# NSA loop in 32 steps of two heads each, and the merge's projection in three split passes

## What is computed

```
q, kv, gates, q_gla, k_gla, v_gla, ..., g_merge = split(rmsnorm(x) @ w_in)
o_a = gate0 * compressed_attention + gate1 * softmax(q_rot k_slc^T) v_slc + gate2 * softmax(q_rot k_win^T) v_win
o_b = rmsnorm(gated linear attention) * silu(r)
gate_a, gate_b = split(sigmoid(g_merge))
merged = gate_a * (o_a @ w_up_nsa) + gate_b * (o_b @ w_up_gla)
x = x + merged @ w_out, then the last SwiGLU layer and the final norm
```

## Time and profile before

| | |
|---|---|
| median of 3 runs | 2349.17 us (2347.92 to 2351.39) |
| the profiled execution's own time | 2335.24 us |
| its span | 2333.4 us |
| mean granted clock of TensorE | 0.981 of full |
| PE busy | 2231.5 us, 96% of the span |
| POOL, DVE, ACT busy | 1146.1, 1003.0, 861.6 us |
| HBM read | 187.92 MB |

### The profile page before, as it was taken

How to read it: one execution, slowest core, us unless ns; L and a number is a source line. 1 busy time by engine, 2 the same in 40 slices (tenths; PEclk the granted TensorE clock), 3 DMA queues, 4 the chain that set the end, 5 groups by cost and what they waited for, 6 DMA issues and landing times.

```text
span 2333.4 us, 28069 instructions
## 1 busy us (share of the span) xinstructions
PE 2231.5 (96%) x10194; PEld 1803.3 (77%) x10194; DVE 1003.0 (43%) x1605; ACT 861.6 (37%) x1239; POOL 1146.1 (49%) x623
## 2 busy tenths in 40 slices
PE   4899989999998999899999999999799999999997
PEld 3788868888886988788888888878556668888886
DVE  5366556422424047744422446353683215331432
ACT  4576744322323223334322334443353224222222
POOL 3777755554554455435554554643101335654552
PEclk9999999999999999999999999999799999999999
DMA  3212213332332222123332332322101223332332
GB/s 131 62 57 62 63 46 100 91 112 85 97 107 67 90 82 73 55 81 104 91 110 88 94 110 77 112 64 73 45 1 46 90 91 91 99 111 84 95 107 73
DMA packets 53251, 193.26 MB, mean 83 GB/s; under 512 B 6816, under 2 KB 7728, under 8 KB 52912
## 3 DMA queue, kind: packets, MB, share of 16 engines
q1 hardware_dynamic: 50688, 184.95, 25.3%
q10 hardware_dynamic: 2480, 7.19, 0.8%
HBM read 187.92 MB, written 4.19 MB: 82 GB/s over the span
## 4 chain that ended last, share of the span: by engine, by line
PE 78%; DVE 9%; ACT 7%; issue 4%; POOL 2%; DMA 0%; SPq 0%; DVEq 0%; ACTq 0%; POOLq 0%
PE ps L367 21%; PE ps L368 20%; PE ps L369 20%; PE ps L934 2%; PE ps L878 2%; PE ps L901 1%; PE ps L572 1%; PE ps L574 1%; PE ps L573 1%; DVE arena L1726 1%; PE ps L458 1%; PE ps L888 1%; ACT w_split L952 1%; PE ps L629 1%; PE ps L631 1%
## 5 line engine op out<-in xcount | busy, mean ns | idle before, releaser
L1401 POOL TENSOR_TENSOR w_split<-ring,w_split 128x1024 fp32r<-128x1024 f32 (+2 forms) x319 | 820.9, 2574 | 1010.7 <-ACT w_split L952 1010.7
L952 ACT CAST w_split<-ring 128x1024 fp32r<-128x1024 f32 (+2 forms) x319 | 347.9, 1091 | 1052.3 <-PE ps L369 931.6
L367 PE MATMUL ps<-u_split,w_split 128*128 128x512 f32 x1768 | 707.5, 400 | 23.8 <-POOL w_split L1401 11.0
L369 PE MATMUL ps<-u_split,w_split 128*128 128x512 f32 x1768 | 694.1, 393 | 0.0
L368 PE MATMUL ps<-u_split,w_split 128*128 128x512 f32 x1768 | 693.5, 392 | 0.0
L367 PEld LDWEIGHTS ps<-u_split,w_split 128*128 128x128 f32 x1768 | 335.3, 190 | 104.2 <-issue 20.4
L369 PEld LDWEIGHTS ps<-u_split,w_split 128*128 128x128 f32 x1768 | 335.0, 189 | 71.4
L368 PEld LDWEIGHTS ps<-u_split,w_split 128*128 128x128 f32 x1768 | 335.5, 190 | 70.1 <-issue 2.9
L367 PE MATMUL ps<-hid,w_split 128*128 128x512 f32 x648 | 254.4, 393 | 2.8 <-DVE arena L1860 2.8
L368 PE MATMUL ps<-hid,w_split 128*128 128x512 f32 x648 | 252.8, 390 | 0.0
L369 PE MATMUL ps<-hid,w_split 128*128 128x512 f32 x648 | 252.7, 390 | 0.0
(11 more groups left out here) (283 smaller groups left out, 2554.4 us busy)
## 6 DMA issues: line engine op xcount, KB each, us to landing
ring<-in_w_hgrn SPq DMA_DIRECT2D x32, 512.0 KB, 3.6
ring<-in_w_attn_qk SPq DMA_DIRECT2D x24, 512.0 KB, 3.6
ring<-in_w_merge SPq DMA_DIRECT2D x24, 512.0 KB, 3.4
ring<-in_w_gu0a SPq DMA_DIRECT2D x22, 512.0 KB, 3.6
ring<-in_w_gu0b SPq DMA_DIRECT2D x22, 512.0 KB, 3.5
ring<-in_w_gu1a SPq DMA_DIRECT2D x22, 512.0 KB, 3.6
ring<-in_w_gu1b SPq DMA_DIRECT2D x22, 512.0 KB, 3.6
ring<-in_w_gu2a SPq DMA_DIRECT2D x22, 512.0 KB, 3.5
```

The source lines that it names most:

```text
L367: nc.tensor.matmul(ps[:, bank], ws[:, 0, r, w], act[:, 0, c], start=c == 0, stop=False)
L369: m = nc.tensor.matmul(ps[:, bank], ws[:, 1, r, w], act[:, 0, c], start=False, stop=c == n - 1)
L952: nc.scalar.copy(ws[:, 0, slot, 0:w], ring[:, r, 0:w]).then_inc(s["w_hi"], 1)
L1401: nc.gpsimd.tensor_tensor(ws[:, 1, slot, 0:w], ring[:, r, 0:w], ws[:, 0, slot, 0:w].bitcast(F32), ALU.subtract).then_inc(s["w_lo"], 1)
```

## The change

The NSA loop has 32 steps (p, x, tt): a pair of heads, a branch and one query tile. The pairs are (0, 5), (1, 4), (2, 7), (3, 6): the first head's features stand in rows 0 to 63, the second's in rows 64 to 127, and one's number is even and the other's odd, so that their values go to different column halves of the array and their outputs to different halves of one bank. The query tiles come in the order 3, 0, 2, 1. A step's scores take one bank for each head; three pairs of banks go round, so scores run two steps ahead, and they wait for the copy of step e-3. In a step VectorE makes one mask addition and one negated maximum for both heads, one reciprocal, and two scalings by two per-partition scalars (reciprocal and gate) in one instruction; ScalarE makes two exponentials and one copy; TensorE two score matmuls, 2(tt+1) transposes and 2(tt+1) value matmuls of 128 columns that alternate between the heads. `nsa_add` runs for both heads of a pair after its eight steps.

In the merge the third unit becomes a split one with 24 passes. `goT` and `oaT` are split once, ScalarE making the hi halves (`outputs_hi`, four inside the loop at steps 4 to 7, two at steps 20 and 22, two after the loop) and GpSimd the lo halves. The staging of the weights in the merge goes from two units for each j to three. Loops of ScalarE and VectorE over the heads are written out.

In the diff old bodies that the listing above shows are left out.

```diff
@@ -61,7 +61,7 @@
...
-PLAIN = [("mid", k) for k, name in enumerate(MID) if name[0] == "w"] + [("merge", 3 * j + 2) for j in range(DC)]
+PLAIN = [("mid", k) for k, name in enumerate(MID) if name[0] == "w"]
...
@@ -226,12 +226,17 @@
...
-        nmax, nneg, nsum, nrec, nw = [take(2, TT) for _ in range(5)]
+        nneg, nsum, nrec = [take(3, 2) for _ in range(3)]
...
+        oa_hi = nc.alloc_sbuf_tensor_at("oa_hi", [P, 4, T], R32, offset=arena_at + 4 * 18 * T)
+        go_hi = nc.alloc_sbuf_tensor_at("go_hi", [P, HEADS_G, T], R32, offset=arena_at + 4 * 44 * T)
+        oa_lo = nc.alloc_sbuf_tensor_at("oa_lo", [P, 4, T], R32, offset=arena_at + 4 * 32 * T)
+        go_lo = nc.alloc_sbuf_tensor_at("go_lo", [P, HEADS_G, T], R32, offset=arena_at + 4 * 28 * T)
...
@@ -240,10 +245,18 @@
...
-        prob, probT = [shared[:, k * 2560:(k + 1) * 2560].rearrange("p (a n) -> p a n", a=2) for k in range(2)]
-        OFF = [0, P, 3 * P, 6 * P]
-        KOFF = [0, 4 * P, 7 * P, 9 * P]
-        BOFF = [0, P, 512, 1024]
+        prob = shared[:, 0:3072].rearrange("p (a h n) -> p a h n", a=3, h=2)
+        probT = shared[:, 3072:5120].rearrange("p (a h n) -> p a h n", a=2, h=2)
+        STEPS = [(p, x, tt) for p in range(HEADS_N // 2) for tt in (3, 0, 2, 1) for x in range(2)]
+        PAIR = [(p, HEADS_N // 2 + (p ^ 1)) for p in range(HEADS_N // 2)]
+        UP_ORDER = (0, 2, 1, 3)
+        OA_DONE = {0: 3, 2: 4, 1: 7, 3: 8}
+        def step_banks(e, n):
+            return ps[:, 2 * (e % 3):2 * (e % 3) + 2, 0:n * P]
...
@@ -867,56 +880,56 @@
             def nsa_scores(e):
...
+                p, x, tt = STEPS[e]
+                if e < 3:
                     pe.wait_ge(s["oa_ready"], 4)
                 else:
...
+                    pe.wait_ge(s["npt_ready"], e - 2)
+                for k, hh in enumerate(PAIR[p]):
+                    rows = slice(k * HD, k * HD + HD)
+                    m = nc.tensor.matmul(step_banks(e, tt + 1)[:, k], q_n[rows, hh % 4, tt * P:(tt + 1) * P],
                                          k_n[rows, x, 0:(tt + 1) * P], start=True, stop=True)
                 m.then_inc(s["ns_ps"], 1)
             def nsa_transposes(e):
...
+                _, _, tt = STEPS[e]
+                for k in range(2):
+                    pe.wait_ge(s["ns_scaled"], 2 * e + k + 1)
+                    for b in range(tt + 1):
+                        m = nc.tensor.transpose(step_banks(e, tt + 1)[:, k, b * P:(b + 1) * P],
+                                                prob[:, e % 3, k, b * P:(b + 1) * P], ident[:])
                 m.then_inc(s["nt_ps"], 1)
             def nsa_values(e):
...
+                p, x, tt = STEPS[e]
+                pe.wait_ge(s["npt_ready"], e + 1)
+                if p >= 2:
+                    pe.wait_ge(s["oa_acc"], 2 * p - 2)
+                for b in range(tt + 1):
+                    for k, hh in enumerate(PAIR[p]):
+                        vcols = slice(x * P + k * HD, x * P + k * HD + HD)
+                        rows = slice(hh % 2 * HD, hh % 2 * HD + HD)
+                        m = nc.tensor.matmul(ps[rows, 6 + p % 2, tt * P:(tt + 1) * P], vsw[:, b, vcols],
+                                             probT[:, e % 2, k, b * P:(b + 1) * P],
+                                             start=x == 0 and b == 0, stop=x == 1 and b == tt)
                 m.then_inc(s["no_ps"], 1)
             pe.wait_ge(s["nrope"], 6)
             pe.wait_ge(s["o_scaled"], HEADS_H + HEADS_G)
...
+            E = len(STEPS)
             nsa_scores(0)
+            nsa_scores(1)
             for e in range(E):
...
+                if e + 2 < E:
+                    nsa_scores(e + 2)
                 nsa_transposes(e)
                 if e:
                     nsa_values(e - 1)
             nsa_values(E - 1)
...
+            pe.wait_ge(s["npt_ready"], E)
             for j in range(DC):
                 b = 4 * (j % 2)
                 pe.wait_ge(s["merged"], j + 1)
@@ -924,15 +937,16 @@
...
-                if j == 0:
-                    pe.wait_ge(s["gb_ready"], HEADS_G)
-                    pe.wait_ge(s["oa_acc"], HEADS_N)
-                rr, v = ring_use("merge", 3 * j + 2)
-                pe.wait_ge(w_ready[rr], v)
-                for c in range(8):
-                    src = oaT[:, c] if c < 4 else goT[:, c - 4]
-                    m = nc.tensor.matmul(ps[:, b + 2 + c // 4], ring[:, rr, c * P:(c + 1) * P], src,
-                                         start=c % 4 == 0, stop=c % 4 == 3)
+                rr, v, _ = split_use("merge", 3 * j + 2)
+                pe.wait_ge(s["w_lo"], v)
+                for n, c in enumerate((4, 5, 6, 7) + UP_ORDER):
+                    if j == 0:
+                        pe.wait_ge(s["up_lo"], n + 1)
+                    up, low = (go_hi, go_lo) if c >= 4 else (oa_hi, oa_lo)
+                    o, w = ps[:, b + 2 + c // 4], slice(c * P, (c + 1) * P)
+                    nc.tensor.matmul(o, ws[:, 0, rr, w], up[:, c % 4], start=n % 4 == 0, stop=False)
+                    nc.tensor.matmul(o, ws[:, 0, rr, w], low[:, c % 4], start=False, stop=False)
+                    m = nc.tensor.matmul(o, ws[:, 1, rr, w], up[:, c % 4], start=False, stop=n % 4 == 3)
...
@@ -1348,37 +1362,49 @@
                 nc.scalar.copy(oaT[:, ft], ps[:, ft]).then_inc(s["oa_ready"], 1)
             act.dma_start(h, a["h_spill"]).then_inc(s["reloaded"], 16)
...
+            def nsa_exps(e):
+                p, x, tt = STEPS[e]
+                act.wait_ge(s["ns_neg"], e + 1)
+                for k in range(2):
+                    nc.scalar.activation(prob[:, e % 3, k, 0:(tt + 1) * P], step_banks(e, tt + 1)[:, k], ACT.Exp,
+                                         bias=nneg[:, e % 3, k:k + 1], accum_out=nsum[:, e % 3, k:k + 1]
                                          ).then_inc(s["ns_exp"], 1)
...
+            def nsa_copies(e):
+                n = STEPS[e][2] + 1
+                act.wait_ge(s["nt_ps"], e + 1)
+                nc.scalar.copy(probT[:, e % 2, :, 0:n * P], step_banks(e, n)).then_inc(s["npt_ready"], 1)
+            def outputs_hi(n):
+                f = n if n < HEADS_G else UP_ORDER[n - HEADS_G]
+                if n < HEADS_G:
+                    act.wait_ge(s["nrope"], 6)
+                    act.wait_ge(s["gb_ready"], f + 1)
+                else:
+                    act.wait_ge(s["oa_acc"], OA_DONE[f])
+                dst, src = (go_hi, goT) if n < HEADS_G else (oa_hi, oaT)
+                nc.scalar.copy(dst[:, f], src[:, f]).then_inc(s["up_hi"], 1)
+            nsa_exps(0)
+            nsa_exps(1)
+            for e in range(len(STEPS)):
+                nsa_copies(e)
+                if e + 2 < len(STEPS):
+                    nsa_exps(e + 2)
+                if 4 <= e < 4 + HEADS_G:
+                    outputs_hi(e - 4)
+                if e in (20, 22):
+                    outputs_hi(HEADS_G + (e - 20) // 2)
+            outputs_hi(HEADS_G + 2)
+            outputs_hi(HEADS_G + 3)
             for j in range(DC):
                 for k in range(2):
...
+                    ahead("merge", 3 * j + k)
                     act.wait_ge(s["mg_raw"], 2 * j + k + 1)
                     nc.scalar.activation(msig[:, 2 * (j % 2) + k], msig[:, 2 * (j % 2) + k], ACT.Sigmoid
                                          ).then_inc(s["mg_sig"], 1)
+                ahead("merge", 3 * j + 2)
                 act.wait_ge(s["m_full"], j + 1)
                 nc.scalar.copy(hid[:, 0, j], mtmp[:, j % 2]).then_inc(s["m_hi"], 1)
             early_norm(6, "mix_out", "gu2a")
@@ -1565,9 +1591,14 @@
...
+            for n in range(2 * HEADS_G):
+                pool.wait_ge(s["up_hi"], n + 1)
+                f = n if n < HEADS_G else UP_ORDER[n - HEADS_G]
+                low, up, src = (go_lo, go_hi, goT) if n < HEADS_G else (oa_lo, oa_hi, oaT)
+                nc.gpsimd.tensor_tensor(low[:, f], src[:, f], up[:, f].bitcast(F32), ALU.subtract).then_inc(s["up_lo"], 1)
...
-                for k in range(2):
-                    lo("merge", 3 * (j + 1) + k) if j + 1 < DC else lo("mix_out", k)
+                for k in range(3):
+                    ahead("merge", 3 * j + k)
...
@@ -2143,61 +2174,44 @@
                 times_sin(x)
                 add_sin(x)
...
+            def nsa_stats(e):
+                n = STEPS[e][2] + 1
+                dve.wait_ge(s["ns_ps"], e + 1)
+                diag = step_banks(e, n)[:, :, (n - 1) * P:n * P]
+                nc.vector.tensor_tensor(diag, diag, res_mask[:, 0:1].broadcast_to((P, 2, P)), ALU.add).then_inc(s["ns_masked"], 1)
+                dve.wait_ge(s["ns_masked"], e + 1)
+                nc.vector.tensor_reduce(nneg[:, e % 3], step_banks(e, n), AX.X, ALU.max, negate=True).then_inc(s["ns_neg"], 1)
+            def nsa_scale(e):
+                p, x, tt = STEPS[e]
+                dve.wait_ge(s["ns_exp"], 2 * e + 2)
+                nc.vector.reciprocal(nrec[:, e % 3], nsum[:, e % 3]).then_inc(s["n_rec"], 1)
```

(48 more changed lines are left out.)

74 lines of the change are left out of this document (removed).

## The result

The changed kernel took a median of 2318.92 us (2311.9 to 2320.88, 4 runs) beside 2350.28 of the kernel before; ratio 0.9868, 95% interval 0.9844 to 0.9892. One of the four executions behind 2350.28 took 2728.23 us and doesn't count in the ratio; the median of the other three is 2349.17. A later comparison on another chip gave 2320.9 beside 2343.99, ratio 0.9906 (0.988 to 0.9932). The forecast's ratio, 2324.6/2349.17 = 0.9895, lies in the second interval and 0.0003 above the first.

The account below looks back on a forecast made before the run. TensorE was taken to bound loop and merge before, VectorE the changed loop: 1.5 + 82 + 8 + 2 = 93 us for 106.2. Loop -13 and merge -11.4 make -24.6 from the median 2349.17: 2324.6 us, range 2316 to 2345.

Parts of the forecast that it names:

- Merge, -11.4: Merge: splitting the third unit saves 1.42 us per column tile, 11.4 us for eight, with the new staging hidden.
- "Zero" for the copies: Loop and merge start: eight hi copies and eight GpSimd low parts cost nothing; without cover up to 6 us once.
- Overlap in issue order, which I take: Loop, TensorE: array halves overlap only partly, between none and full; group 10.5 us, loop 84.
- rival 1: Loop: full overlap and no stalls, VectorE's floor, 85.5 us; total 2317; chance 0.15.
- TensorE's lower bound of 71 us: Loop, TensorE: with full overlap of the array's halves a group takes 8.9 us, the loop 71.
- VectorE is the new floor: Loop: VectorE's work, 10.3 us a group and 82 us in all, sets the loop's time.
- I allow 0.25 us a step: Loop: estimated stalls where wide steps meet narrow ones in the ring of three bank pairs, 8 us in all.
- It just fits: Loop ring: an average step's 2.3 us until its statistics can start is covered by VectorE's 2.4 us of queued work.
- Rival 2: Loop: no overlap, TensorE bounds again, 113 us; total 2344.7; chance 0.15.
- Rival 3: Loop: stalls eat the gain, the ring bounds at 3.2 us a step; total 2337; chance 0.08.
- Rival 4: Merge: staging is late through GpSimd's subtraction, so the merge gives nothing; total 2336; chance 0.03.
- Rival 5: Loop: TensorE's clock falls to half; half the loop so gives 2352.6, all of it 2386; chance 0.07.

Follow-up runs that it names:

- merge_only: Kernel before with only the merge's third unit split; old 16-step loop kept, copies of finished outputs between its steps; 2345.69 us, ratio 0.9999 to before.
- no_mask: Changed kernel without the 32 causal-mask additions on VectorE; 2315.26 us (one run), loop 85.5 us.
- split_quiet: Changed kernel with ScalarE's copy split per head and the output copies moved ahead of and behind the loop's steps; 2314.36 us, ratio 0.9857 to before.
- no_overlap: Changed kernel with heads paired so both use the same half of the array; 2340.14 us, ratio 0.9981 to before.
- quiet_pool: Changed kernel with the copies of outputs moved ahead of and behind the loop's steps, so GpSimd is silent beside them; 2324.88 us, ratio 0.9895 to before.
- filler: Changed kernel with a needless 128x128 matmul on TensorE before each step's scores; 2324.7 us, ratio 0.9924 to before.

## Why the prediction was right, and where not

The time was right, and the local gain too, 22.8 us for 24.6. The merge's half came by the forecast's own mechanism. The loop's half, -13.4 for -13.2, was luck: the engine named as the floor wasn't it, and two errors cancelled.

- **Merge, -11.4:** right. 16.3 us a tile, no idle before the third unit, -11.1. What it missed is the end: VectorE's last addition beside a GpSimd subtraction that wasn't there before costs 1.39 us once.
- **"Zero" for the copies:** nearly right for this kernel's places, where three subtractions cost eight steps 0.5 us (22.21 for 21.72), wrong as a statement on cover. In merge_only the same sixteen instructions, between the last steps of the old loop, took back all 11 us, more than the 6 that the forecast named as its bound. The price came through VectorE's scalings and through more time at half clock, not through late staging.
- **"Overlap in issue order, which I take":** this step failed. The halves overlap in full, 0.055 us a pass. The rule behind rival 1, the Trainium skill's TensorEngine Tiling (Array Packing), section Tiling Modes, is borne out. TensorE's lower bound of 71 us was near the 75.2 measured, part of which is half clock; the 84 taken wasn't. And 84 stood above VectorE's 82: by its own figures the forecast should have called TensorE the floor.
- **"VectorE is the new floor", 82:** failed in size. It is busy 73.6 us and waits about 17 (15.7 for scores, 1.2 for exponentials), so it needs 75.5. At equal clock, taking 2.8 us of work off it shortened eight steps by 1.4 only (no_mask). Most of the surplus is the reciprocal: 0.32 with its hand-over by the earlier trace rows, 0.19 measured (1724.06 to 1724.25), 4 us in 32 steps. The last row measured the gap to a dependent multiplication that the new loop doesn't have.
- **"I allow 0.25 us a step" for the ring, 8:** the right mechanism, undersized. "It just fits" was wrong: 82 and 11 around it were forecast, 75.5 + 17 = 92.5 came, the 17 with what the half-clock stretches add. Two errors of 6 us with opposite signs made the forecast's 93 look better than it was.
- **Rival 1** (no stalls, 85.5) had its premise right and its conclusion not: full overlap moved the wait from TensorE to the ring. split_quiet is the kernel that nearly gets there. **Rival 2** was measured as no_overlap: 111.8 for the 113 named, and a median 6.5 us under before. **Rival 3** is the mechanism that binds, at 92.5/32 = 2.9 us a step instead of 3.2. **Rival 4** didn't occur.
- **Rival 5**, the clock: it occurred, in small. The Trainium skill's TensorE: Matmul & The Clock Gate, section A second HAM failure mode: psum-queue depth-cycling, has small idle gaps make the clock oscillate, and in the steady loop it did fall, one to three times, for at most 7 us each. The forecast's "1.00 after the first 15 us" is wrong. A fall of 7 us costs 2.3 (quiet_pool); the rival needed three whole groups of four steps at half clock. That three was itself too low: it counts 8.1 us a group from TensorE's 10.5, but the forecast's group took 93/8 = 11.6, so 7.0 are lost and it takes three and a half; and all of the loop at half clock gives some 2384 by the same sum, not 2386.

## What to carry to other kernels

When an engine is relieved by an overlap, ask next how long one turn of the buffer ring is, link by link, and not which engine has the most work: here a copy started one head earlier gave 3 to 4 us that no engine's busy time showed. Cover on GpSimd isn't free for VectorE work next to it, so place it where neither is awaited. Measure a local change by cutting the profiles at fixed instructions, and compare stretches with the same granted clock; the whole time of one run hid 9 us of unrelated shifts, and the loop's own length up to 3 us of half clock.

## What the runs showed of the hardware

- f32 matmuls on two row halves (64x128) or two column halves (128x64) of the array run fully side by side, 0.055 us per 128-column pass for 0.107, although each is two passes on the same half. A change of the array's shape costs 0.15 to 0.21 us.
- VectorE is slowed by GpSimd's work on SBUF next to it: an addition of 128x512 takes 2.69 us beside a GpSimd subtraction and 0.69 alone; a step's four scalings take 3.29 us beside two subtractions and 1.27 alone.
- TensorE's clock fell from 2.4 to 1.2 GHz for 3 to 7 us at a time well inside loops in which TensorE waited in every step, and not in filler and no_mask, whose TensorE waits less, nor in no_overlap's steady loop. In quiet_pool's loop, which TensorE doesn't bound, 7 us at half clock cost 2.3.
